# Q of the odd heads in four more block pairs, x convolved beside the z pairs, and a head loop of six weight chunks in a new order

## What is computed

```python
h = rmsnorm(x, pre_norm_g)
q, k, v, z_attn, z_ssm, xbc, dt_raw = jnp.split(h @ w_in, cuts, axis=-1)   # 16 heads x 128 for q, k, v, z_attn
o = dilated_attention(q, k, v, rel_bias_table)                             # three dilated windows, merged
attn_out = rmsnorm(o, attn_norm_g) * jax.nn.silu(z_attn)
xbc = jax.nn.silu(conv(xbc, conv_w) + conv_b)                              # depthwise, width 5, centred
y = ssd_scan(xs, dt_f, a_f, bm, cm) + reversed scan + d_skip * xs          # chunks of 128 tokens
ssm_out = rmsnorm_by_group(y * jax.nn.silu(z_ssm))
out = x + rmsnorm(concat([attn_out, ssm_out]) @ w_out, post_norm_g)
```

## Time and profile before

| | |
|---|---|
| runs | 2431.27 us median of 3 (2430.18 to 2431.59) |
| profiled execution | 2428.37 us; its span, first to last instruction, 2426.6 us |
| PE busy | 2402.4 us, 99% of the span, 13700 matmuls |
| DVE, ACT, POOL busy | 1739.3 (72%), 976.6 (40%), 386.0 us (16%) |
| prologue, pairs, heads, output | to 254, to 1135, to about 1932, to 2427 us |
| granted clock of PE | 0.999 |
| HBM | 159 GB/s over the span |

### The profile page before, as it was taken

The page is one execution under the profiler, slowest core; times in us unless marked ns, Lnnn a source line. Parts: engine busy times, 40 slices in busy tenths (PEclk is TensorE's granted clock), DMA queues, the critical chain, the costliest instruction groups (busy, mean ns, idle before and its releaser), DMA issues.

```text
span 2426.6 us, 37095 instructions
## 1 busy us (share of the span) xinstructions
PE 2402.4 (99%) x13700; PEld 2282.6 (94%) x13700; DVE 1739.3 (72%) x2436; ACT 976.6 (40%) x1611; POOL 386.0 (16%) x580
## 2 busy tenths in 40 slices
PE   7999999999999999999999999999999999999998
PEld 6999999999999999999999999999999988888887
DVE  5686766666666655554787888888888868787767
ACT  6333433333333333333445444544554533333332
POOL 0000276666666600000000000000000000000000
PEclk9999999999999999999999999999999999999999
DMA  4235466666666533335464546554554445444544
GB/s 164 79 108 175 130 188 190 187 192 192 185 188 185 177 95 95 96 103 201 150 187 146 180 138 187 179 151 138 185 178 137 130 134 182 150 156 135 172 166 157
DMA packets 318777, 380.22 MB, mean 157 GB/s; under 512 B 21623, under 2 KB 239031, under 8 KB 315752
## 3 DMA queue, kind: packets, MB, share of 16 engines
q1 hardware_dynamic: 265207, 222.06, 30.1%
q10 hardware_dynamic: 35056, 106.81, 13.4%
q0 software_dynamic: 18432, 50.36, 6.4%
HBM read 299.95 MB, written 86.55 MB: 159 GB/s over the span
## 4 chain that ended last, share of the span: by engine, by line
PE 96%; DMA 1%; DVE 1%; ACT 1%; issue 0%; SPq 0%; ACTq 0%; DVEq 0%
PE ps L1039 36%; PE ps L836 21%; PE ps L1188 14%; PE ps L814 8%; PE ps L1112 5%; PE ps L998 2%; PE ps L964 2%; PE ps L931 2%; PE ps L947 1%; PE ps L1008 1%; DMA w_raw<-in_w_in 1%; PE ps L764 0%; PE ps L971 0%; PE ps L850 0%; PE ps L938 0%; PE ps L981 0%
## 5 line engine op out<-in xcount | busy, mean ns | idle before, releaser
L1039 PE MATMUL ps<-h_hi,w_hi 128*128 128x384 f32 x960 | 322.2, 336 | 0.0
L1039 PE MATMUL ps<-h_lo,w_hi 128*128 128x384 f32 x960 | 322.0, 335 | 0.0
L1039 PE MATMUL ps<-h_hi,w_lo 128*128 128x384 f32 x960 | 321.7, 335 | 0.0
L2237 DVE TENSOR_TENSOR w_lo<-raw_qk,w_hi 128x512 fp32r<-128x512 f32 x240 | 180.7, 754 | 183.7 <-ACT w_hi L1563 182.7
L836 PE MATMUL ps<-h_hi,w_hi 128*128 128x384 f32 x1056 | 273.7, 340 | 1.2 <-DVE w_lo L1848 1.2
L836 PE MATMUL ps<-h_lo,w_hi 128*128 128x384 f32 x1056 | 268.9, 335 | 0.0
L836 PE MATMUL ps<-h_hi,w_lo 128*128 128x384 f32 x1056 | 268.8, 335 | 0.0
L1265 ACT ACTIVATE w_hi<-w_raw 128x512 fp32r<-128x512 f32 x172 | 107.5, 628 | 393.0 <-PE ps L836 205.0
L1039 PE MATMUL ps<-t_hi,w_lo 128*128 128x384 f32 x720 | 243.5, 338 | 0.0
L1039 PE MATMUL ps<-t_hi,w_hi 128*128 128x384 f32 x720 | 243.2, 338 | 0.0
L1039 PE MATMUL ps<-t_lo,w_hi 128*128 128x384 f32 x720 | 242.6, 337 | 0.0
(11 more groups left out here) (342 smaller groups left out, 5128.2 us busy)
## 6 DMA issues: line engine op xcount, KB each, us to landing
raw_qk<-in_w_in SPq DMA_DIRECT2D x90, 512.0 KB, 4.3
w_raw<-in_w_in SPq DMA_DIRECT2D x176, 256.0 KB, 3.7
stage<-loc_scr ACTq DMA_DIRECT2D x16, 1536.0 KB, 7.5
stage<-t_scr SPq DMA_DIRECT2D x48, 512.0 KB, 3.7
stage<-in_w_out SPq DMA_DIRECT2D x36, 512.0 KB, 3.7
stage<-zx_scr ACTq DMA_DIRECT2D x46, 384.0 KB, 9.1
stage<-in_w_in SPq DMA_DIRECT2D x30, 512.0 KB, 4.3
u_scr<-stage ACTq DMA_DIRECT2D x32, 384.0 KB, 2.6
```

Source lines behind the costliest of these rows:

```text
L1039: ins = nc.tensor.matmul(ps[:, bank, 0:HALF_T], w, h(k), start=(start and kk == 0 and q == 0), stop=(last and kk == KC - 1 and q == 2), sk ...
L2237: nc.vector.tensor_tensor(w_lo[:, n_slot(n, pp), :], src, w_hi[:, n_slot(n, pp), :].bitcast(f32), ALU.subtract).then_inc(w_lo_done, 1)
```

## The change

- Z_P moves from 15 to 19: **four more pairs** (`"qq"`) stand between the x pairs and the z pairs and make Q of heads 1, 3, ... 15. NP is 34.
- **x of heads 1 to 15 is convolved beside the z pairs.** POOL loads a tile of x from `zx_scr` into `tap_a` and `tap_b`, DVE applies the five taps into PSUM banks 6 and 7 (`convolve_tile`, at halves 4, 5, 6, 7, 9 of the pair), ACT takes the SiLU at half 12, POOL stores the tile again. `tap_a` and `tap_b` lie where POOL's sums for `w_out` have their buffers, and POOL does the tiles after these sums. Head 0 is still convolved at the start of the heads.
- **The stream** is K of head 0, then K of the odd and Q and K of the even heads, then the two gate tiles of head 15: 100 chunks instead of 132. A head is six chunks, twelve halves of 12 matmuls (`stream_half`).
- **The order of a head is new on all engines** (`head`): PE does the work of slot 7 of the last head after half 1, both scores after half 3, both turned probabilities after half 7, probabilities times V and x turned after half 8, V turned after half 10, the SSD across chunks after half 12. ACT loads the decays at the head's start, and Q of the next odd head behind the bias strip. The loops over heads are unrolled.
- SP loads the first chunk of K of head 0 only when POOL's last tile of x is stored.

The diff, cut to its core:

```diff
+STREAM = [("k", 0)]
+for _i in range(1, HEADS):
+    STREAM += [("k", _i)] if _i % 2 else [("q", _i), ("k", _i)]
+STREAM += [("za", HEADS - 1), ("zs", HEADS - 1)]
-IT_CHUNKS = TILES * NCH
+IT_CHUNKS = 6
-XS_P, Z_P = 1 + V_PAIRS, 1 + V_PAIRS + XS_PAIRS
+QQ_PAIRS = 4
+XS_P = 1 + V_PAIRS
+QQ_P = XS_P + XS_PAIRS
+Z_P = QQ_P + QQ_PAIRS
+TAP_AT = {4: 0, 5: 1, 6: 2, 7: 3, 9: 4}
+        tap_a = sq_c[:, P:P + HALF_T + 4]
+        tap_b = stage[:, T_LO[1] + HT + HW:T_LO[2]]
+        xc_in, XC_IN = sum_d_in, 32 * SUM_TURNS
 ...
+            for i in range(2):
+                pool.wait_ge(sum_a_out[i], 16 * SUM_TURNS)
+            pool.wait_ge(sum_d_out, 32 * SUM_TURNS)
+            nc.gpsimd.memset(tap_a[:, 0:2], 0.0).then_inc(sum_done, 1)
 ...
+            for h in range(1, HEADS):
+                rows = zx_scr[(ZX_XS + h) * P:(ZX_XS + h + 1) * P, :]
+                if h > 1:
+                    pool.wait_ge(xc_out, XC_OUT + 48 * (h - 1))
+                pool.dma_start(tap_a[:, 2:HALF_T + 4], rows[:, 0:HALF_T + 2]).then_inc(xc_in, 16)
 ...
+                pool.wait_ge(xc_silu, XC_SILU + h)
+                pool.dma_start(rows[:, 0:HALF_T], tap_a[:, 2:HALF_T + 2]).then_inc(xc_out, 16)
 ...
-            sp.wait_ge(sum_d_out, 32 * SUM_TURNS)
+            sp.wait_ge(xc_out, XC_OUT + 48 * (HEADS - 1))
 ...
+            def head(a):
+
+                stream_halves(a, 0, 1)
+                if a > 0:
+                    within_chunks(a - 1)
+                stream_halves(a, 1, 2)
+                scores(a)
+                scores_of_sample(a)
+                stream_halves(a, 3, 4)
+                turn_probs(a)
+                turn_probs_of_sample(a)
+                stream_halves(a, 7, 1)
+                attend(a)
+                turn_x(a)
+                stream_halves(a, 8, 2)
+                if a < LAST:
+                    turn_v(a + 1)
+                stream_halves(a, 10, 2)
+                across_chunks(a)
 ...
+            def load_behind_scores(a):
+                if a < LAST:
+                    load_strip(a + 1)
+                    if a % 2 == 0:
+                        act.wait_ge(sscores_ready, a + 1)
+                        act.dma_start(raw_qk[:, T:2 * T], zx_scr[(ZX_Q + a + 1) * P:(ZX_Q + a + 2) * P, :]
+                                      ).then_inc(q0_in, 16)
 ...
+                exp_of_scores(a)
+                load_behind_scores(a)
+                stream_hi(m)
+                q_rounded(i)
+                stream_hi(m + 1)
+                stream_hi(m + 2)
+                probs_rounded(a)
 ...
+            def convolve_tile(h, k):
+                if k == 0:
+                    dve.wait_ge(xc_in, XC_IN + 48 * h)
```

More of the change, by code:

```diff
@@ new lines, in turn_x @@
+            def turn_x(a):
+                if a == 0:
+                    pe.wait_ge(xs_silu, 1)
+                else:
+                    pe.wait_ge(xs_in, XS_IN + 16 * a)
+                for half, bank in ((0, 7), (1, 4)):
+                    for q in range(3):
+                        c = 3 * half + q
+                        last = nc.tensor.transpose(ps[:, bank, q * P:(q + 1) * P],
+                                                   x_of(a)[:, c * P:(c + 1) * P], ident)
+                    last.then_inc(xt_ready, 1)
@@ new lines, in turn_v @@
+            def turn_v(i):
+                pe.wait_ge(v_in, 16 * i + 16)
+                if i > 0:
+                    pe.wait_ge(o_out, 2 * i)
+                for half, bank in ((0, 5), (1, 6)):
+                    for q in range(3):
+                        c = 3 * half + q
+                        last = nc.tensor.transpose(ps[:, bank, q * P:(q + 1) * P],
+                                                   vT[:, c * P:(c + 1) * P], ident)
+                    last.then_inc(vt_ready, 1)
@@ new lines, in within_chunks @@
+            def within_chunks(a):
+                pe.wait_ge(off_read, 2 * a + 1)
+                pe.wait_ge(wmat_done, a + 1)
+                for c in range(TT):
+                    b, o = (5, c) if c < PCH else (6, c - PCH)
+                    for h in range(2):
+                        last = nc.tensor.matmul(
+                            ps[64 * h:64 * h + 64, b, o * P:(o + 1) * P],
+                            x_tok[:, c * P + 64 * h:c * P + 64 * h + 64],
+                            decay[:, h * T + c * P:h * T + (c + 1) * P], start=True, stop=True)
+                    if c in (PCH - 1, TT - 1):
+                        last.then_inc(diag_ready, 1)
@@ L1610, in pair @@
                     half_hi(p, pp, n)
+                    if n == 12 and h > 0:
+                        silu_of_tile(h)
                     if n == 2 and not first:
@@ L1632, in _ @@
             pair(1, 1)
-            with act.Fori(1, NP // 2) as g:
+            with act.Fori(1, Z_P // 2) as g:
                 pair(2 * g, 0)
                 pair(2 * g + 1, 1)
+            for p in range(Z_P // 2 * 2, NP):
+                pair(p, p % 2, p - Z_P + 1)
             def split_first(m):
@@ L1669, in w2_split @@
+            for a in range(HEADS - 1):
+                head(a)
             def w2_split(u):
@@ L2319, in pair @@
                     half_lo(p, pp, n)
+                    if n in TAP_AT and h > 0:
+                        convolve_tile(h, TAP_AT[n])
                     if n == 0:
```

903 lines of the change are left out of this document (488 added, 415 removed).

## The result

The change is slower: 2496.36 us median of 4 runs (2491.57 to 2500.52), before on the same chip 2431.43 (2430.18 to 2431.78). The ratio is 1.027, 95% interval 1.0257 to 1.0282, so 65 us more, where 52 were forecast. The profiled execution took 2497.7 us with a span of 2495.9, 69.3 us more than the span of before.

What follows compares the result with a forecast made beforehand. PE's own work was taken as the bound. Terms -16.6, +32, +1, +2, +18.5, +13.5 and +1.8 sum to +52 us, 2483 us on the median, range 2465 to 2505, taken out to 2448 and 2512.

Steps and rivals of the forecast that it cites:

- Fewer matmuls: Whole kernel: 32 fewer stream chunks save 134.1 us, four more pairs cost 117.5; net -16.6 us.
- POOL's wait: First z pair, pair 19: PE waits for DVE's tap, whose data POOL loads after its w_out sums; +32 us.
- refilling DVE's lead: Behind the wait in pair 19: DVE gets ahead of PE again; +1 us.
- x beside the z pairs: z pairs: DVE's 5.5 us more per pair still fits, so the arithmetic costs nothing.
- Turned probabilities: All 16 heads: the second sequence's four transposes wait 1.16 us for DVE's first read of bank 4; +18.5 us.
- Q as a load: Even heads: Q lands late in ACT's queue, 4 us more in heads 4, 8, 12, 1 to 2 in head 0; +13.5.
- The output: End of the heads: PE waits about one piece for the output's first operand; +1.8 us.
- The clock behind long waits: Pair 19: PE restarts at a lower clock after the long wait; +2 us, with heads' shorter waits left to the range.
- the first (the head loop paced by DVE and the loads): Heads: each waits 2 us more at a tight hand-over, +32 us, giving 2515 us; chance 0.13.
- Rivals 2 to 5: Pair 19 and heads: one or both waits absent or cheap; 2451 (0.10), 2448 (0.07), 2416 (0.05), within 5 us (0.02).

Runs made afterwards that it cites:

- the version without waits: Also called the last version: the change with seven edits to waits, loads, POOL's semaphores and the order at the output; 2423.74 us, ratio 0.9965 to before.
- the two experiments that mend Q: Two edits of the change: Q's load issued ahead of the strip (2467.93 us); Q rounded behind the turned probabilities (2467.98 us).
- The dose: Waits put into the version without waits: second sequence's transposes directly behind the sixteen, 2440.12 us; these also waiting for DVE's last read, 2487.67 us.
- POOL's denser turns: The change with separate semaphores for POOL's fourth buffer, so the third is reloaded while the fourth is summed and stored; 2467.48 us.

## Why the prediction was right, and where it fell short

The direction, the order of size and both places were right: one gap in pair 19 and a wait in front of L1023 in every head. By its steps:

- *Fewer matmuls*, -16.6: it holds, by the busy time of the version without waits, within 1.1 us.
- *POOL's wait*, +32: 26.4. The end was forecast at 855.4 and was 852.18, as POOL's sums ended 3 us earlier than in the earlier trace rows although they began 3 us later; and PE came to half 5 at 825.8 and not 822.8. The gain of 1 to 4 us that I named and left out was there. That POOL's late sums are the cause is shown: with them done earlier the gap is gone. The +1 for refilling DVE's lead was nothing.
- *x beside the z pairs* costs nothing: the pairs behind the gap are full.
- *Turned probabilities*, +18.5, and *Q as a load*, +13.5: 36.7 together for 32. The odd heads waited 0.87 to 1.12 us where 1.16 was worked out from the earlier trace rows. Heads 4, 8 and 12 waited 6.0, 5.1 and 4.9 for the 5.2 of the sum. Head 0 waited 7.1 instead of 2 to 3: I had Q's load there but not the stream's weights, which come as late; 6.0 and 5.2 us of wait stay there in the two experiments that mend Q.
- *The output*, +1.8: 1.8.
- *The clock behind long waits*, **+2: this is the step that failed**. In pair 19 it was right (2.5), but the sum had no such term for the heads and the output, and there it was 13.7 us. "No row here shows a gap of that length in mid-kernel" was true, yet the row at the kernel's end already showed the clock going down within an idle time of 6 us, and for PE a wait of 5 us is idle time as well. The dose shows that it goes down behind 2.7 us too, in twelve of fifteen cases. The rule that I had weighed, in the Trainium skill (TensorE: Matmul & The Clock Gate, HAM oscillation), that a gap throttles the array and each one is paid again, is borne out by the 24 waits of over 3 us, and only in part by the shorter ones. I had priced it at 5 us for three heads; six places paid it, at 1.7 to 3.0 us, and two of them had waited only 2.3 and 2.0 us. Which of the waits of 2 to 3 us are paid looks like chance as far as these traces go, so of the 13.7 us some 3.4 (head 10 and the output) could have been absent in another execution.

Sum by these steps: 52.2 forecast, -5.6 and -1 at POOL, +4.7 in the heads, +0.5 and +13.7 for the clock, +1.6 for the rest of the busy time, +3.4 for the early spell: 69.5, for the 69.3 of the profiled executions. So the near hit of the total, 2496 for 2483, hides errors of both signs: 6.6 too much at POOL, and some 24 too little elsewhere, more than half of it the clock. The range was narrower than the ends of its own terms, too, which add up to some 2455 and 2520.

Of the rivals the first (the head loop paced by DVE and the loads) had this in its favour, that hand-overs with a margin under 2 us were lost where a load was late; but a clean head is 41.4 us, as forecast, and in the last version the heads run with 0.3 us of waits, so they aren't paced by DVE. Rivals 2 to 5 each wanted at least one of the two waits gone or at a third of its price, and both stood.

## What to carry to other kernels

Price an idle time of the matmul engine with the slow restart behind it, wherever it stands: here 1.4 to 3.5 us behind every wait of over 3 us, and 1.4 to 1.7 behind most of those of 2 to 3 us, so that one of 2.7 us mostly cost half as much again as it lasted. Two short waits close together counted as a long one in one place. When work is moved to an engine that is idle "later", look up when it becomes free and who stands behind the wait, and ask of every wait put in a queue what is queued behind it: here a few moved lines and two semaphores turned +65 us into -7.5.

## What the runs showed of the hardware

- The clock's fall isn't decided by the length of the wait alone: behind equal waits of 2.67 us it fell in most heads and not in head 11, a low spell lasts 3.4 us or about twice that, and one of 3.4 or 6.8 us came at about 89 us in all variants with PE busy throughout, behind 44 small products of 32 columns that are also there before. Why it is spared there in the profiled execution of before stays open.
- POOL's sums slow DVE. Between 300 and 720 us the same DVE subtraction (two inputs in SBUF) takes 810 ns in the change and 891 with POOL's denser turns, and 691 behind 900 us, where POOL is nearly idle; an addition with one input in PSUM stays at 554:

```profile
L2399 DVE TENSOR_TENSOR w_lo<-raw_qk,w_hi 128x512 fp32r<-128x512 f32 x117 | 94.8, 810 | 86.5 <-ACT w_hi L1657 86.0
...
L2408 DVE TENSOR_TENSOR w_raw<-w_raw,ps 128x384 f32<-128x384 f32 x29 | 16.1, 554 | 24.5 <-PE ps L1111 24.5
```

```profile
L2410 DVE TENSOR_TENSOR w_lo<-raw_qk,w_hi 128x512 fp32r<-128x512 f32 x115 | 101.5, 891 | 60.1 <-ACT w_hi L1668 59.3
...
L2419 DVE TENSOR_TENSOR w_raw<-w_raw,ps 128x384 f32<-128x384 f32 x29 | 16.1, 554 | 21.3 <-PE ps L1122 21.1
```

```profile
L2399 DVE TENSOR_TENSOR w_lo<-raw_qk,w_hi 128x512 fp32r<-128x512 f32 x92 | 63.6, 691 | 36.7 <-ACT w_hi L1657 36.3
```

The Trainium skill (GPSIMD Engine Reference, Specifications) names contention on the shared SBUF interfaces for DVE instructions with two SBUF inputs; these rows agree. The DMA traffic isn't the reason: in the heads, with POOL at rest and the DMA engines nearly as busy (their share is 0.55 there, 0.62 between 300 and 720 us), the subtraction takes 681 ns. One by one, the subtractions of 300 to 720 us that overlap one of POOL's additions take 1036 ns on average in the change, the others 689 and never over 693. POOL is slowed as well: its additions take 932 ns on average beside DVE's work and 711 to 735 in the gap, where DVE stands still. That is part of why its sums ended sooner there; its loads of `w_out` landed sooner too, after 2.6 us and not 3.2.
